# Moving a norm out of the delta rule's pair boundaries, and half panels ahead of the SSD diagonals

## The chip, the cores and the metric

The kernel runs on one core of a Trainium2 chip. The metric is the device time of one execution in microseconds, the median over several. The core has five engines, each with its own instruction queue, kept in step by semaphores: TensorE (PE in the profile, its weight loads PEld), VectorE (DVE), ScalarE (ACT), GpSimd (POOL) and SyncE (SP, which issues the DMAs here).

## The reference

Two transformer blocks over 512 tokens of width 1024. The change is in the mixer of the second block, which projects its input, runs a gated delta rule over 8 heads and an SSD (Mamba-2) scan over 16 heads, and joins both:

```python
z = h @ w_in                     # split into q, k, v, z_a, ..., z_s, x_s, b_s, c_s, dt_s
qkv = silu(causal_dwconv(concat([q, k, v]), gdn_conv_w))
o_a = gdn_chunked(q, k, v, g, beta)                    # 8 heads of 128
o_a = rms_norm(o_a, gdn_norm_w) * silu(z_a)            # mean of squares over a head's 128
xbc = silu(causal_dwconv(concat([x_s, b_s, c_s]), ssd_conv_w, ssd_conv_b))
y = ssd_chunked(xs, dt, a_neg, bm, cm) + ssd_d * xs    # 16 heads of 64
o_s = rms_norm(y * silu(z_s), ssd_norm_w)
mix = concat([o_a, o_s]) @ w_out
```

The norm of `o_a` needs, for each head and token, the sum of 128 squares, a root, an inverse, and this one number spread over the head's 128 rows.

## The kernel before

Everything is kept transposed: 128 channels on the partitions, 512 tokens along the free dimension. A projection goes panel by panel. A panel is 128 output channels: 8 blocks of depth, each multiplied three times (upper weights by upper input, upper by lower, lower by upper), so 24 matmuls of 128x512 into one PSUM bank. SP loads a panel's raw weights, ACT rounds them to the upper part (`upper_part`, L471), DVE subtracts to the lower part (`lower_parts`, L455); four panels are in flight (`RING`), and the banks `ps0` to `ps3` rotate.

The order on each engine is the order of the code. In the second block's mixer PE runs `gdn_project_pe` (24 panels with small work behind them), `gdn_pe`, the 12 panels of `ssd_xbc` and one of `ssd_dt`, `ssd_pe`, `y_turn_pe`, the 8 panels of `ssd_z`, then `out2_pe`.

`gdn_pe`, `gdn_act`, `gdn_dve` and `gdn_pool` are the delta rule. They take the 8 heads two at a time (four pairs); for each pair they go through a list of stages, each stage for the one head and then for the other. `PE_STAGES` is: `bc` (spread the head's decays and betas over the partitions), `kk` (products of keys with keys and with queries), `t0` and the six levels of a blocked inversion (`x`, `u`, `t` for each), `w`, the scan over four chunks (`v`, `s`), then `ss` and `bk`. ACT has `dec` (the decays, Exp), `small`, copies, then `sq` (keeps the output, and squares it) and `rt` (root). DVE has `kb`, `at`, `qk`, the levels, the states, then `inv` and `out`. `after(engine, stage, n)` gives the semaphore count at which a stage of head n is through. The norm of a pair's output stands at the pair's end:

- ACT `sq` (L1697, L1698) squares; PE `ss` (L1656) sums over the partitions with four matmuls of one column; ACT `rt` (L1703) takes four roots for a head; DVE `inv` (L1754) inverts; PE `bk` spreads over 128 rows by `spread` (L634: four 128x128 matmuls); DVE `out` (L1757) multiplies.
- The next pair's first stage, `bc`, waits for `out` of the head two before it.

The profile counts a float32 matmul as two instructions, so `ss` of two heads is x16, and so is `spread` of two heads.

`ssd_pe` first runs `ssd_prepare_pe` (turns blocks of `xbc`, with halves of the panels 0 to 2 of `gdn_z` in between: `z_half_pe`, L1794 to L1796, 12 matmuls for a half panel). Then for each of 16 heads: PE `broadcast` (L1894, L428), ACT four Exp (L1961), DVE the mask product (L1990), PE `diag` (L1903), ACT keeps (L1954). A half panel of `gdn_z` stands behind `diag(n)` for the six n in `Z_IN_DIAG`. `z_keep_dve`, `z_upper_act` and `z_silu_act` handle these panels, on DVE behind heads 6 and 11, on ACT behind heads 2, 7 and 12 (upper parts) and 8 (Silu).

Of the kernel before, what the change touches and what calls it, by code (L numbers as in the profile page):

```python
# [126 lines left out]
def build(nc, T, stop_at=None):  # L127
# [1381 lines left out]
    NL = len(LEVELS)  # L1509
    lev = [(k, l) for l in range(NL) for k in ("x", "u", "t") if k != "t" or l < NL - 1]  # L1510
    scan = [(k, c) for c in range(QB) for k in ("v", "s")]
    PE_STAGES = ["bc", "kk", "t0"] + lev + ["w"] + scan + ["ss", "bk"]
    ACT_STAGES = ["dec", "small", "t0"] + [x for x in lev if x[0] != "u"] + ["w"] + [("v", c) for c in range(QB)] + ["sq", "rt"]
    DVE_STAGES = ["kb", "at", "qk"] + [("u", l) for l in range(NL - 1)] + ["full", ("u", NL - 1)] + [("s", c) for c in range(QB)] + ["inv", "out"]
    POOL_STAGES = ["q", "vb"] + [("c", l) for l in range(NL - 1)] + ["kbe", "kd"]
    STAGES = {"pe": PE_STAGES, "act": ACT_STAGES, "dve": DVE_STAGES, "pool": POOL_STAGES}

    def after(eng, stage, n):

        order_ = STAGES[eng]  # L1520
        return n // 2 * 2 * len(order_) + 2 * order_.index(stage) + n % 2 + 1

    def slots(n):

        return [solve_t[:, n % 2, k, :] for k in range(6)]

    def heads_in_turn(stages):
        for n2 in range(4):
            for stage in stages:
                for n in (2 * n2, 2 * n2 + 1):  # L1530
                    yield stage, stage[0] if isinstance(stage, tuple) else stage, n

    def packed(x, half):

# [10 lines left out]
        return qkv[:, 8 + n, :]  # L1545

    def gdn_pool(pool):
        for stage, what, n in heads_in_turn(POOL_STAGES):
            vb, kt = chunks(qkv[:, 16 + n, :]), chunks(ktok[:, n, :])
            if stage == "q":  # L1550

                pool.wait_ge(g_act, after("act", "dec", n))
                pool.wait_ge(g_pe, after("pe", "kk", n))
                pool.tensor_tensor(qkv[:, n, :], qkv[:, n, :], slots(n)[3], ALU.mult).then_inc(g_pool, 1)
                continue
            if stage == "vb":
# [16 lines left out]
            pool.tensor_tensor(packed(*level_part(n, l)), packed(slots(n)[0], 0),  # L1573
                               per_chunk(cst[:, C_LEV + (l + 1) * 64:C_LEV + (l + 2) * 64]), ALU.mult).then_inc(g_pool, 1)

    def gdn_pe(pe):
        for stage, what, n in heads_in_turn(PE_STAGES):
            At, Tm, U, X, C, QK = slots(n)
            B = [ps[4 * (n % 2) + k] for k in range(4)]
            q, k, vb, kd = qkv[:, n, :], qkv[:, 8 + n, :], qkv[:, 16 + n, :], ktok[:, n, :]  # L1580
# [2 lines left out]
            if stage == "bc":  # L1583

                if n >= 2:
                    pe.wait_ge(g_dve, after("dve", "out", n - 2))
                else:
                    pe.wait_ge(small_act, 2)
                    pe.wait_ge(small_dve, 2)
# [40 lines left out]
            elif stage == "w":  # L1630
                pe.wait_ge(g_dve, after("dve", ("u", NL - 1), n))
                pe.wait_ge(g_pool, after("pool", "kbe", n))
                for c in range(QB):
                    mm = pe.matmul(B[0][:, cc[c]], C[:, cc[c]], U[:, cc[c]], start=True, stop=True)
            elif what == "v":
                c = stage[1]
                if c == 0:
                    pe.wait_ge(g_act, after("act", "w", n))
                    pe.wait_ge(g_pool, after("pool", "kd", n))
                else:  # L1640
                    pe.wait_ge(g_dve, after("dve", ("s", c - 1), n))
                mm = pe.matmul(B[1][:, cc[c]], U[:, cc[c]], vb[:, cc[c]], start=True, stop=c == 0)
                if c:
                    mm = pe.matmul(B[1][:, cc[c]], X[:, cc[c]], S, start=False, stop=True)
            elif what == "s":
                c = stage[1]
                pe.wait_ge(g_act, after("act", ("v", c), n))
                if c:
                    pe.matmul(B[2][:, cc[c]], S, q[:, cc[c]], start=True, stop=False)
                mm = pe.matmul(B[2][:, cc[c]], Tm[:, cc[c]], QK[:, cc[c]], start=c == 0, stop=True)  # L1650
                if c < QB - 1:
                    mm = pe.matmul(B[3][:, cc[c]], kd[:, cc[c]], Tm[:, cc[c]], start=True, stop=True)
            elif stage == "ss":
                pe.wait_ge(g_act, after("act", "sq", n))
                for c in range(QB):
                    mm = pe.matmul(B[0][:, c:c + 1], X[:, cc[c]], ones[:, 0:1], start=True, stop=True)  # L1656
            elif stage == "bk":
                pe.wait_ge(g_dve, after("dve", "inv", n))
                mm = spread(pe, B[1], stat[:, 48 + 4 * (n % 2):52 + 4 * (n % 2)], QB)
            mm.then_inc(g_pe, 1)  # L1660

    def gdn_act(act):
        for stage, what, n in heads_in_turn(ACT_STAGES):
            At, Tm, U, X, C, QK = slots(n)
            B = [ps[4 * (n % 2) + k] for k in range(4)]
            cc = [slice(c * P, (c + 1) * P) for c in range(QB)]
# [25 lines left out]
            elif what == "v":  # L1692
                act.wait_ge(g_pe, after("pe", stage, n))
                x = act.activation(Tm[:, cc[stage[1]]], B[1][:, cc[stage[1]]], ACT.Copy)
            elif stage == "sq":
                act.wait_ge(g_pe, after("pe", ("s", QB - 1), n))
                act.activation(qkv[:, n, :], B[2][:, :], ACT.Copy)  # L1697
                x = act.activation(X, B[2][:, :], ACT.Square)  # L1698
            elif stage == "rt":
                act.wait_ge(g_pe, after("pe", "ss", n))  # L1700
                for c in range(QB):
                    o = 40 + 4 * (n % 2) + c
                    x = act.activation(stat[:, o:o + 1], B[0][:, c:c + 1], ACT.Sqrt, bias=QEPS[:, c, n:n + 1], scale=1.0 / 128)  # L1703
            x.then_inc(g_act, 1)

    def gdn_dve(dve, st):
        for stage, what, n in heads_in_turn(DVE_STAGES):
            At, Tm, U, X, C, QK = slots(n)
            B = [ps[4 * (n % 2) + k] for k in range(4)]
            q, k = qkv[:, n, :], qkv[:, 8 + n, :]  # L1710
# [31 lines left out]
            elif what == "s":  # L1742
# [6 lines left out]
                                                 op0=ALU.mult, op1=ALU.add)  # L1749
                else:  # L1750
                    x = dve.tensor_copy(stat[:, 92:93], stat[:, 95:96])
            elif stage == "inv":
                dve.wait_ge(g_act, after("act", "rt", n))
                x = dve.reciprocal(stat[:, 48 + 4 * (n % 2):52 + 4 * (n % 2)], stat[:, 40 + 4 * (n % 2):44 + 4 * (n % 2)])  # L1754
            elif stage == "out":
                dve.wait_ge(g_pe, after("pe", "bk", n))
                x = dve.scalar_tensor_tensor(out=q, in0=q, scalar=v(V_GDN), in1=B[1][:, :], op0=ALU.mult, op1=ALU.mult)  # L1757
            x.then_inc(g_dve, 1)
            dve.wait_ge(g_dve, after("dve", stage, n))

# [93 lines left out]

    s_turn_in = [xbc[:, b, :] for b in range(10)]
    s_turn_out = [xt[:, b, :] for b in range(10)]
    Z_IN_DIAG = {1: (3, 0), 4: (3, 1), 6: (4, 0), 9: (4, 1), 11: (5, 0), 14: (5, 1)}
    Z_IN_STATE = ((6, 0), (6, 1), (7, 0), (7, 1))

    def ssd_prepare_pe(pe):  # L1860
# [25 lines left out]
    def ssd_pe(pe):  # L1886
# [23 lines left out]
        for n in range(16):  # L1910
            if 1 <= n < 15:
                broadcast(n + 1)
            diag(n)
            if n in Z_IN_DIAG:
                z_half_pe(pe, *Z_IN_DIAG[n])
        for c in range(QB):
            for g in range(2):
                e = 2 * c + g
# [342 lines left out]
    with block as blk:  # L2261
# [28 lines left out]
        def _(pe):  # L2290
# [31 lines left out]
            gdn_project_pe(pe)  # L2322
            pe.wait_ge(tok2_done, 16)
            gdn_pe(pe)
            pe.wait_ge(g_dve, after("dve", "out", 7))
            for name in ("ssd_xbc", "ssd_dt"):
                multiply(pe, name, u_of(u_hi), u_of(u_lo))
            ssd_pe(pe)
            y_turn_pe(pe)
            multiply(pe, "ssd_z", u_of(u_hi), u_of(u_lo))  # L2330
# [8 lines left out]
        def _(act):  # L2339
# [73 lines left out]
        def _(dve):  # L2413
# [113 lines left out]
```

## Time and profile before

| | |
|---|---|
| median of 3 runs | 2531.75 us (2530.27 to 2535.05) |
| the profiled execution: time, span | 2535.12 us, 2533.3 us |
| PE busy, share of the span | 2428.6 us, 96% |
| DVE busy | 1340.2 us, 53% |
| ACT busy | 886.5 us, 35% |
| POOL busy | 120.7 us, 5% |
| mean granted TensorE clock | 0.973 |

Times inside the trace are microseconds from the start of the span. The granted clock is given as a share of 2.4 GHz: 1.00 is 2.4 GHz, 0.50 is 1.2 GHz, and a value in between is a stretch that had some of each. PE's busy time counts matmuls that overlap in its pipeline, so the start of one matmul to the start of the next is what a matmul costs in a stream. A timeline row may merge several instructions; x16 says how many.

### The profile page before, as it was taken

Reading aid. Unit: us, or ns where it says so; the run is one execution under the profiler, and the core shown is the slowest. Engines: PE = TensorE matmul, PEld = TensorE weight load, DVE = VectorE, ACT = ScalarE, POOL = GpSimd, SP = SyncE. Lnnn points to the kernel's source line nnn. Section 1 sums busy time; section 2 is a strip of 40 time slices with the busy share of each in tenths; the row PEclk is TensorE's granted clock in tenths of the full one; section 3 lists DMA queues with packets and bytes.
Section 4 is the critical chain, followed back from the end, with each engine's and each line's share of the span. In section 5 each row is a group of like instructions: output and inputs, shape, how many; then the busy total and the mean of one; then the engine's idle time right before and its main releaser. Section 6 shows DMA issues by size and latency. Waiting matters only on the chain.

```text
span 2533.3 us, 31667 instructions
## 1 busy us (share of the span) xinstructions
PE 2428.6 (96%) x12764; PEld 1900.3 (75%) x12764; DVE 1340.2 (53%) x2037; ACT 886.5 (35%) x1480; POOL 120.7 (5%) x156
## 2 busy tenths in 40 slices
PE   7999999999999999999999999888998999999997
PEld 6888888887556658888888667677876687788886
DVE  5454335436466557544533586344464754777623
ACT  4222223321344455322222454443345243433321
POOL 0000000000012220000000000233000000000000
PEclk9999999999999999999999999898998999999998
DMA  5333324330221125333333232000031232333331
GB/s 168 100 93 97 98 80 137 97 83 17 76 66 59 39 71 171 88 100 93 99 98 82 80 91 76 2 2 2 27 85 34 58 100 67 92 92 100 99 95 48
DMA packets 372465, 200.02 MB, mean 79 GB/s; under 512 B 12000, under 2 KB 364512, under 8 KB 372320
## 3 DMA queue, kind: packets, MB, share of 16 engines
q1 hardware_dynamic: 372320, 198.01, 27.1%
q8 instruction: 101, 1.65, 0.3%
q14 instruction: 44, 0.36, 0.0%
HBM read 190.38 MB, written 7.60 MB: 78 GB/s over the span
## 4 chain that ended last, share of the span: by engine, by line
PE 91%; DVE 6%; ACT 2%; issue 1%; POOL 0%; DMA 0%; DVEq 0%; SPq 0%; ACTq 0%; POOLq 0%
PE ps L522 19%; PE ps L523 19%; PE ps L524 19%; PE ps L376 2%; PE ps L1025 2%; PE ps L1433 2%; PE ps L1435 2%; PE ps L1434 2%; PE ps L1061 2%; PE ps L378 2%; PE ps L377 2%; PE ps L2137 1%; PE ps L2139 1%; PE ps L2138 1%; PE ps L912 1%
## 5 line engine op out<-in xcount | busy, mean ns | idle before, releaser
L455 DVE TENSOR_TENSOR w_lo<-w_raw,w_hi 128x1024 fp32r<-128x1024 f32 (+2 forms) x366 | 422.7, 1156 | 310.4 <-ACT w_hi L471 309.2
L522 PE MATMUL ps<-u_hi,w_hi 128*128 128x512 f32 (+1 forms) x1416 | 557.5, 394 | 3.0 <-DVE w_lo L455 2.1
L523 PE MATMUL ps<-u_lo,w_hi 128*128 128x512 f32 (+1 forms) x1416 | 555.0, 392 | 0.0
L524 PE MATMUL ps<-u_hi,w_lo 128*128 128x512 f32 (+1 forms) x1416 | 554.6, 392 | 0.0
L471 ACT ACTIVATE w_hi<-w_raw 128x1024 fp32r<-128x1024 f32 (+2 forms) x366 | 366.2, 1002 | 502.5 <-PE ps L524 438.4
L522 PEld LDWEIGHTS ps<-u_hi,w_hi 128*128 128x128 f32 (+1 forms) x1416 | 264.2, 187 | 64.3 <-DVE w_lo L455 3.0
L524 PEld LDWEIGHTS ps<-u_hi,w_lo 128*128 128x128 f32 (+1 forms) x1416 | 264.2, 187 | 60.9 <-issue 1.5
L523 PEld LDWEIGHTS ps<-u_lo,w_hi 128*128 128x128 f32 (+1 forms) x1416 | 264.1, 187 | 60.4 <-issue 2.2
L524 PE MATMUL ps<-mid_hi,w_lo 128*128 128x512 f32 x528 | 208.6, 395 | 0.0
L522 PE MATMUL ps<-mid_hi,w_hi 128*128 128x512 f32 x528 | 208.6, 395 | 0.0
L523 PE MATMUL ps<-mid_lo,w_hi 128*128 128x512 f32 x528 | 208.5, 395 | 0.0
L523 PEld LDWEIGHTS ps<-mid_lo,w_hi 128*128 128x128 f32 x528 | 99.1, 188 | 24.2
L524 PEld LDWEIGHTS ps<-mid_hi,w_lo 128*128 128x128 f32 x528 | 99.1, 188 | 24.0
L522 PEld LDWEIGHTS ps<-mid_hi,w_hi 128*128 128x128 f32 x528 | 99.1, 188 | 24.0
L646 ACT ACTIVATE pair_a<-pair_a 128x512 f32<-128x512 f32 x44 | 27.9, 635 | 214.6 <-DVE pair_a L655 214.6
L1126 POOL TENSOR_TENSOR probs<-probs,stat 128x256 f32<-128x256 f32 (+1 forms) x80 | 56.1, 706 | 871.6 <-DVE stat L1135 871.6
L660 DVE TENSOR_TENSOR part<-ps,pair_b 128x512 f32<-128x512 f32 x44 | 30.4, 692 | 126.6 <-PE ps L524 126.5
L376 PE MATMUL ps<-u_hi,w_hi 128*128 128x512 f32 x192 | 89.3, 465 | 0.0
L1309 DVE SCALAR_TENSOR_TENSOR conv_t<-conv_in,vec,conv_t 128x512 f32<-128x512 f32 x108 | 81.0, 750 | 9.0 <-ACT conv_t L1291 6.4
L2223 ACT ACTIVATE conv_t<-conv_in,vec 128x512 f32<-128x512 f32 x44 | 36.0, 818 | 138.9 <-DVE conv_in L2238 138.9
L655 DVE TENSOR_TENSOR pair_a<-ps,rms 128x512 f32<-128x512 f32 x44 | 30.4, 691 | 95.5 <-PE ps L524 95.4
L378 PE MATMUL ps<-u_hi,w_lo 128*128 128x512 f32 x192 | 77.4, 403 | 0.0
(440 smaller groups left out, 3680.9 us busy)
## 6 DMA issues: line engine op xcount, KB each, us to landing
w_raw<-w_in_dram SPq DMA_DIRECT2D x101, 512.0 KB, 3.8
w_raw<-ffn_w_gate_dram SPq DMA_DIRECT2D x44, 512.0 KB, 3.8
w_raw<-ffn_w_up_dram SPq DMA_DIRECT2D x44, 512.0 KB, 3.8
w_raw<-w_up_dram SPq DMA_DIRECT2D x44, 512.0 KB, 3.8
w_raw<-ffn_w_down_dram SPq DMA_DIRECT2D x32, 512.0 KB, 4.0
w_raw<-w_out_dram SPq DMA_DIRECT2D x24, 512.0 KB, 3.8
w_raw<-w_down_dram SPq DMA_DIRECT2D x16, 512.0 KB, 3.7
w_raw<-ffn_w_down_dram SPq DMA_DIRECT2D x16, 384.0 KB, 3.4
```

The costliest lines, as they stand in the source:

```text
L376: pe.matmul(out, wh, u_hi[:, k, :], start=k == 0, stop=False)
L377: pe.matmul(out, wh, u_lo[:, k, :], start=False, stop=False)
L378: mm = pe.matmul(out, wl, u_hi[:, k, :], start=False, stop=k == DK - 1)
L455: dve.tensor_tensor(lo, raw, hi.bitcast(F32), ALU.subtract).then_inc(w_split, 1)
L471: act.activation(w_hi[:, n % RING, 0:blocks, 0:cols], w_raw[:, n % RING, 0:blocks, 0:cols], ACT.Copy).then_inc(hi_done, 1)
L522: pe.matmul(out, wh, h_k, start=k0 + k == 0, stop=False)
L523: pe.matmul(out, wh, l_k, start=False, stop=False)
L524: mm = pe.matmul(out, wl, h_k, start=False, stop=end)
L1025: mm = pe.matmul(bank[:, 0:w], j.q[:, q * P:(q + 1) * P], j.k[:, 0:w], start=True, stop=plain)
L1061: mm = pe.matmul(out[:, j.first[t]:SEQ], j.v[t], x, start=t == 0, stop=t == nk - 1)
L1126: pool.tensor_tensor(x, x, r, ALU.mult).then_inc(sc_norm, 1)
L1309: dve.scalar_tensor_tensor(out=t, in0=x, scalar=v(wcol + block(n) * taps + k), in1=t, op0=ALU.mult, op1=ALU.add).then_inc(conv_done if k = ...
```

## The change

Four things are done.

1. The stages `ss` and `bk` leave the end of PE's list. `ss` of heads n-2 and n-1 is now issued behind `kk` of the pair n, n+1, writes into the bank B[1], and reads squares that `sq` puts into `upper(n)` and no longer into X. `bc` waits for `sq` of the head two before, not for `out`.
2. `rt`, `inv` and `out` are gone from the stage lists. DVE has a stage `mean` behind `qk` of the next pair: one instruction on 128x4 numbers for a head, that adds sum/128 to `QEPS`. The last pair's `ss` and `mean` stand by themselves at the end. One root (`o_root_act`) and one reciprocal (`o_inverse_dve`) then serve all eight heads (128x32).
3. The panels of `ssd_xbc` get a loop of their own (`xbc_pe`): behind each of the first eight panels one head's `spread` is issued, into ps6 or ps7, and behind that panel's convolution on DVE the multiplication (`o_norm_dve`) of that head.
4. In the SSD, the half panels of `gdn_z` are issued ahead of `diag(n)`, not behind it, and the first one at n = 0 where it was 1.

```diff
-    PE_STAGES = ["bc", "kk", "t0"] + lev + ["w"] + scan + ["ss", "bk"]
-    ACT_STAGES = ["dec", "small", "t0"] + [x for x in lev if x[0] != "u"] + ["w"] + [("v", c) for c in range(QB)] + ["sq", "rt"]
-    DVE_STAGES = ["kb", "at", "qk"] + [("u", l) for l in range(NL - 1)] + ["full", ("u", NL - 1)] + [("s", c) for c in range(QB)] + ["inv", "out"]
+    PE_STAGES = behind(["bc", "kk", "t0"] + lev + ["w"] + scan, ("kk", "ss"))
+    ACT_STAGES = ["dec", "small", "t0"] + [x for x in lev if x[0] != "u"] + ["w"] + [("v", c) for c in range(QB)] + ["sq"]
+    DVE_STAGES = behind(["kb", "at", "qk"] + [("u", l) for l in range(NL - 1)] + ["full", ("u", NL - 1)] + [("s", c) for c in range(QB)],
+                        ("qk", "mean"))
+    NEXT_PAIR = ("ss", "mean")
+    TURNS = {eng: [(stage, n) for pair in range(5) for stage in stages
+                   for n in (2 * pair, 2 * pair + 1) for n in (n - 2 if stage in NEXT_PAIR else n,) if 0 <= n < 8]
+             for eng, stages in STAGES.items()}
...
                 if n >= 2:
-                    pe.wait_ge(g_dve, after("dve", "out", n - 2))
+                    pe.wait_ge(g_act, after("act", "sq", n - 2))
...
             elif stage == "ss":
-                pe.wait_ge(g_act, after("act", "sq", n))
+                pe.wait_ge(g_act, after("act", "dec", n + 2) if n < 6 else after("act", "sq", n))
                 for c in range(QB):
-                    mm = pe.matmul(B[0][:, c:c + 1], X[:, cc[c]], ones[:, 0:1], start=True, stop=True)
-            elif stage == "bk":
-                pe.wait_ge(g_dve, after("dve", "inv", n))
-                mm = spread(pe, B[1], stat[:, 48 + 4 * (n % 2):52 + 4 * (n % 2)], QB)
+                    mm = pe.matmul(B[1][:, c:c + 1], upper(n)[:, cc[c]], ones[:, 0:1], start=True, stop=True)
...
-                x = act.activation(X, B[2][:, :], ACT.Square)
-            elif stage == "rt":
-                act.wait_ge(g_pe, after("pe", "ss", n))
-                for c in range(QB):
-                    o = 40 + 4 * (n % 2) + c
-                    x = act.activation(stat[:, o:o + 1], B[0][:, c:c + 1], ACT.Sqrt, bias=QEPS[:, c, n:n + 1], scale=1.0 / 128)
+                x = act.activation(upper(n), B[2][:, :], ACT.Square)
...
-            elif stage == "inv":
-                dve.wait_ge(g_act, after("act", "rt", n))
-                x = dve.reciprocal(stat[:, 48 + 4 * (n % 2):52 + 4 * (n % 2)], stat[:, 40 + 4 * (n % 2):44 + 4 * (n % 2)])
-            elif stage == "out":
-                dve.wait_ge(g_pe, after("pe", "bk", n))
-                x = dve.scalar_tensor_tensor(out=q, in0=q, scalar=v(V_GDN), in1=B[1][:, :], op0=ALU.mult, op1=ALU.mult)
+            elif stage == "mean":
+                dve.wait_ge(g_pe, after("pe", "ss", n))
+                x = dve.scalar_tensor_tensor(out=QEPS[:, :, n], in0=B[1][:, 0:QB], scalar=1.0 / 128, in1=QEPS[:, :, n], op0=ALU.mult, op1=ALU.add)
...
+    def o_root_act(act):
+        act.wait_ge(g_dve, after("dve", "mean", 7))
+        act.activation(o_means, o_means, ACT.Sqrt).then_inc(o_rt, 1)
+
+    def o_inverse_dve(dve):
+        dve.wait_ge(o_rt, 1)
+        dve.reciprocal(o_means, o_means).then_inc(o_inv, 1)
+
+    def o_spread_pe(pe, n):
+        pe.wait_ge(o_inv, 1)
+        if n >= 2:
+            pe.wait_ge(o_normed, n - 1)
+        spread(pe, ps[6 + n % 2], QEPS[:, :, n], QB).then_inc(o_bc, 1)
+
+    def o_norm_dve(dve, n):
+        if n < 8:
+            x = o_a[:, n, :]
+            dve.wait_ge(o_bc, n + 1)
+            dve.scalar_tensor_tensor(out=x, in0=x, scalar=v(V_GDN), in1=ps[6 + n % 2][:, :], op0=ALU.mult, op1=ALU.mult).then_inc(o_normed, 1)
...
+    def xbc_pe(pe):
...
+            mm.then_inc(w_used, 1)
+            if p < 8:
+                o_spread_pe(pe, p)
...
-    Z_IN_DIAG = {1: (3, 0), 4: (3, 1), 6: (4, 0), 9: (4, 1), 11: (5, 0), 14: (5, 1)}
+    Z_IN_DIAG = {0: (3, 0), 4: (3, 1), 6: (4, 0), 9: (4, 1), 11: (5, 0), 14: (5, 1)}
...
-            diag(n)
             if n in Z_IN_DIAG:
                 z_half_pe(pe, *Z_IN_DIAG[n])
+            diag(n)
...
-            pe.wait_ge(g_dve, after("dve", "out", 7))
-            for name in ("ssd_xbc", "ssd_dt"):
-                multiply(pe, name, u_of(u_hi), u_of(u_lo))
+            pe.wait_ge(g_dve, after("dve", "mean", 7))
+            xbc_pe(pe)
+            multiply(pe, "ssd_dt", u_of(u_hi), u_of(u_lo))
...
             gdn_act(act)
+            o_root_act(act)
...
-            conv_dve(dve, "ssd_xbc", 24, 4, V_SCW)
+            o_inverse_dve(dve)
+            conv_dve(dve, "ssd_xbc", 24, 4, V_SCW, lambda p: o_norm_dve(dve, p))
```

## Rows read from the trace of the kernel before

**Rows 1.** The page, chain of work that ended last: shares by engine.

```profile
PE 91%; DVE 6%; ACT 2%; issue 1%; POOL 0%; DMA 0%; DVEq 0%; SPq 0%; ACTq 0%; POOLq 0%
```

**Rows 2.** Timeline between second and third pair: start, duration, engine, line, operation, count, idle before.

```profile
1691.67 2.03 PE L1656 MATMUL ps<-cst,solve_t 128*128 128x1 f32 x16 [0.54 <-ACT solve_t L1698]
1691.99 0.62 ACT L1698 ACTIVATE solve_t<-ps 128x512 f32<-128x512 f32 x1
1692.62 1.28 ACT L1703 ACT_TABLE_LOAD   x1
1694.97 3.46 PE L634 MATMUL ps<-cst,stat 128*128 128x128 f32 x16 [1.26 <-DVE stat L1754]
1698.26 0.38 PE L1590 MATMUL ps<-cbf 128*128 128x512 bf16 x1
1699.33 0.60 ACT L1670 ACTIVATE solve_t<-ps 128x512 f32<-128x512 f32 x1 [2.79 <-PE ps L428]
```

**Rows 3.** Chain of waits, the two other boundaries: start, duration, what.

```profile
1636.68 0.49 ACT solve_t L1698
...
1646.04 0.60 ACT solve_t L1670
...
1745.31 0.60 ACT qkv L1697
...
1755.26 0.60 ACT solve_t L1670
```

**Rows 4.** Timeline from the last pair's end into `ssd_xbc`.

```profile
1801.53 0.62 ACT L1698 ACTIVATE solve_t<-ps 128x512 f32<-128x512 f32 x1
...
1804.28 0.18 DVE L1754 RECIPROCAL stat<-stat 128x4 f32<-128x4 f32 x1 [3.34 <-ACT stat L1703]
...
1809.20 0.79 PE L522 MATMUL ps<-u_hi,w_hi 128*128 128x512 f32 x1 [0.91 <-DVE qkv L1757]
...
1814.04 0.40 PE L524 MATMUL ps<-u_hi,w_lo 128*128 128x512 f32 x1
...
1817.45 0.39 PE L524 MATMUL ps<-u_hi,w_lo 128*128 128x512 f32 x1
```

**Rows 5.** Windows: length, busy times of PE, PEld, DVE, ACT, POOL; PEclk, DMA, GB/s.

```profile
1810.00:1812.00 2.00, 2.00 (x6) 1.51 (x6) 0.00 (x0) 0.00 (x0) 0.00 (x0) 0.50 0.00 0
...
1820.00:1875.00 55.00, 55.00 (x244) 45.56 (x243) 39.62 (x52) 23.53 (x31) 0.00 (x0) 1.00 0.33 89
...
1902.00:1904.00 2.00, 2.00 (x14) 1.67 (x13) 1.97 (x4) 1.99 (x4) 0.00 (x0) 1.00 0.00 0
...
1944.00:1946.00 2.00, 2.00 (x8) 1.71 (x8) 1.26 (x3) 0.38 (x1) 0.00 (x0) 0.50 0.00 0
```

**Rows 6.** Timeline, the same spread of two heads inside `out2`.

```profile
2052.87 1.95 PE L634 MATMUL ps<-cst,stat 128*128 128x128 f32 x16
...
2054.57 0.47 PE L2137 MATMUL ps<-oa_hi,w_hi 128*128 128x512 f32 x1
```

**Rows 7.** Groups by line in 1809 to 1882, the convolution's steps on DVE.

```profile
L1309 DVE SCALAR_TENSOR_TENSOR conv_t<-conv_in,vec,conv_t 128x512 f32<-128x512 f32 x36 | 27.0, 750 | 1.5 <-ACT conv_t L1291 0.7
```

**Rows 8.** Timeline of the SSD diagonals.

```profile
1903.17 5.77 DVE L1981 TENSOR_TENSOR xt<-xt,sv 128x512 f32<-128x512 f32 x8
...
1912.86 1.83 PE L1903 MATMUL ps<-xt,pair_b 128*128 128x64 f32 x8 [3.48 <-DVE pair_b L1990]
...
1917.46 1.05 ACT L471 ACTIVATE w_hi<-w_raw 128x1024 fp32r<-128x1024 f32 x1
...
1921.10 0.39 PE L1894 MATMUL ps<-cbf 128*128 128x512 bf16 x1
1921.54 1.00 PE L1903 MATMUL ps<-xt,pair_b 128*128 128x64 f32 x8
...
1942.80 1.97 PE L1903 MATMUL ps<-xt,pair_b 128*128 128x64 f32 x8 [3.65 <-DVE pair_b L1990]
...
1948.58 0.39 PE L1894 MATMUL ps<-cbf 128*128 128x512 bf16 x1
```

More of the change, by code:

```diff
@@ L1511, in build, with behind, heads_in_turn @@
     scan = [(k, c) for c in range(QB) for k in ("v", "s")]
-    PE_STAGES = ["bc", "kk", "t0"] + lev + ["w"] + scan + ["ss", "bk"]
-    ACT_STAGES = ["dec", "small", "t0"] + [x for x in lev if x[0] != "u"] + ["w"] + [("v", c) for c in range(QB)] + ["sq", "rt"]
-    DVE_STAGES = ["kb", "at", "qk"] + [("u", l) for l in range(NL - 1)] + ["full", ("u", NL - 1)] + [("s", c) for c in range(QB)] + ["inv", "out"]
+    def behind(stages, *later):
+        out = []
+        for stage in stages:
+            out += [stage] + [x for spot, x in later if spot == stage]
+        return out
+    PE_STAGES = behind(["bc", "kk", "t0"] + lev + ["w"] + scan, ("kk", "ss"))
+    ACT_STAGES = ["dec", "small", "t0"] + [x for x in lev if x[0] != "u"] + ["w"] + [("v", c) for c in range(QB)] + ["sq"]
+    DVE_STAGES = behind(["kb", "at", "qk"] + [("u", l) for l in range(NL - 1)] + ["full", ("u", NL - 1)] + [("s", c) for c in range(QB)],
+                        ("qk", "mean"))
     POOL_STAGES = ["q", "vb"] + [("c", l) for l in range(NL - 1)] + ["kbe", "kd"]
     STAGES = {"pe": PE_STAGES, "act": ACT_STAGES, "dve": DVE_STAGES, "pool": POOL_STAGES}
+    NEXT_PAIR = ("ss", "mean")
+    TURNS = {eng: [(stage, n) for pair in range(5) for stage in stages
+                   for n in (2 * pair, 2 * pair + 1) for n in (n - 2 if stage in NEXT_PAIR else n,) if 0 <= n < 8]
+             for eng, stages in STAGES.items()}
+    PLACE = {(eng, stage, n): i + 1 for eng, turns in TURNS.items() for i, (stage, n) in enumerate(turns)}
     def after(eng, stage, n):
-        order_ = STAGES[eng]
-        return n // 2 * 2 * len(order_) + 2 * order_.index(stage) + n % 2 + 1
+        return PLACE[eng, stage, n]
     def slots(n):
         return [solve_t[:, n % 2, k, :] for k in range(6)]
[L1527 to L1531, printed above, removed]
+    def heads_in_turn(eng):
+        for stage, n in TURNS[eng]:
+            yield stage, stage[0] if isinstance(stage, tuple) else stage, n
     def packed(x, half):
@@ L1547, in gdn_pool @@
     def gdn_pool(pool):
-        for stage, what, n in heads_in_turn(POOL_STAGES):
+        for stage, what, n in heads_in_turn("pool"):
             vb, kt = chunks(qkv[:, 16 + n, :]), chunks(ktok[:, n, :])
@@ L1576, in gdn_pe @@
     def gdn_pe(pe):
-        for stage, what, n in heads_in_turn(PE_STAGES):
+        for stage, what, n in heads_in_turn("pe"):
             At, Tm, U, X, C, QK = slots(n)
@@ L1653, in gdn_pe @@
             elif stage == "ss":
-                pe.wait_ge(g_act, after("act", "sq", n))
+                pe.wait_ge(g_act, after("act", "dec", n + 2) if n < 6 else after("act", "sq", n))
                 for c in range(QB):
-                    mm = pe.matmul(B[0][:, c:c + 1], X[:, cc[c]], ones[:, 0:1], start=True, stop=True)
-            elif stage == "bk":
-                pe.wait_ge(g_dve, after("dve", "inv", n))
-                mm = spread(pe, B[1], stat[:, 48 + 4 * (n % 2):52 + 4 * (n % 2)], QB)
+                    mm = pe.matmul(B[1][:, c:c + 1], upper(n)[:, cc[c]], ones[:, 0:1], start=True, stop=True)
             mm.then_inc(g_pe, 1)
     def gdn_act(act):
-        for stage, what, n in heads_in_turn(ACT_STAGES):
+        for stage, what, n in heads_in_turn("act"):
             At, Tm, U, X, C, QK = slots(n)
@@ L1697, in gdn_act @@
                 act.activation(qkv[:, n, :], B[2][:, :], ACT.Copy)
-                x = act.activation(X, B[2][:, :], ACT.Square)
-            elif stage == "rt":
-                act.wait_ge(g_pe, after("pe", "ss", n))
-                for c in range(QB):
-                    o = 40 + 4 * (n % 2) + c
-                    x = act.activation(stat[:, o:o + 1], B[0][:, c:c + 1], ACT.Sqrt, bias=QEPS[:, c, n:n + 1], scale=1.0 / 128)
+                x = act.activation(upper(n), B[2][:, :], ACT.Square)
             x.then_inc(g_act, 1)
     def gdn_dve(dve, st):
-        for stage, what, n in heads_in_turn(DVE_STAGES):
+        for stage, what, n in heads_in_turn("dve"):
             At, Tm, U, X, C, QK = slots(n)
@@ L1758, in gdn_dve @@
             x.then_inc(g_dve, 1)
             dve.wait_ge(g_dve, after("dve", stage, n))
+    o_rt, o_inv, o_bc, o_normed = (sem("o_" + n) for n in ("root", "inverse", "spread", "normed"))
+    o_means = QEPS.rearrange("p c h -> p (c h)")
+    def o_root_act(act):
[4 more added lines that the diff above has]
+        dve.reciprocal(o_means, o_means).then_inc(o_inv, 1)
@@ new lines, in o_spread_pe @@
+    def o_spread_pe(pe, n):
[9 more added lines that the diff above has]
+    def xbc_pe(pe):
+        s = segs["ssd_xbc"]
+        for p in range(12):
+            n = s.base + p
+            pe.wait_ge(w_split, n + 1 + RING)
+            pe.wait_ge(bank_read, s.group + p + 1)
+            out = ps[(s.group + p) % BANKS][:, :]
+            for k in range(DK):
+                wh, wl = w_hi[:, n % RING, k, :], w_lo[:, n % RING, k, :]
+                pe.matmul(out, wh, u_hi[:, k, :], start=k == 0, stop=False)
+                pe.matmul(out, wh, u_lo[:, k, :], start=False, stop=False)
+                mm = pe.matmul(out, wl, u_hi[:, k, :], start=False, stop=k == DK - 1)
+            mm.then_inc(w_used, 1)
+            if p < 8:
+                o_spread_pe(pe, p)
```

## The prediction

> **What bounds the kernel now.** I read the page's chain first: 91% of it is PE, 6% DVE, 2% ACT [rows 1]. So almost everywhere PE's stream is the time, and what can be won is where PE stands still or runs at the lower clock. The mixer of the second block has such places, and the change touches two kinds of them.
>
> The first is the end of each pair of heads in the delta rule. In the timeline between the second and third pair [rows 2] the reader sees a relay: ACT's last square ends at 1692.61, PE sums, ACT loads the root's table (1.28), DVE inverts, PE spreads (from 1694.97, 16 instructions in 3.46), DVE multiplies, and only then does PE start the next pair's broadcasts (1698.26) and ACT its decays (1699.33). The chain of waits shows the same at the two other boundaries [rows 3]. At the end of the last pair the relay goes from 1802.15 to 1809.20, where the projection `ssd_xbc` starts [rows 4]. Its first 11 matmul spacings, from 1809.20 to 1814.04, are 0.44 us each; 15 later ones, to 1817.45, are 0.227. The windows say why: granted clock 0.50 in 1810 to 1812, which is 1.2 GHz, after an engine that had largely waited [rows 5].
>
> The second is the SSD's diagonals. PE is idle for 3.48 us ahead of the first `diag` (1912.86) and for 3.65 ahead of the one at 1942.80 (ACT is then busy with the Silu of the z panels, between two table loads), and each time it works at 1.2 GHz for a while behind the gap [rows 5, 8].
>
> **Part 1: the three boundaries between pairs.** `bc` will wait for `sq` of the head two before. That is done where `ss` starts now, 1691.67. From `bc`'s first matmul to the decays it takes 1699.33 - 1698.26 = 1.07 [rows 2]. So the decays start at 1692.74 (ACT is free from 1692.61) and not at 1699.33: 6.6 us. At the first boundary the first square ends at 1636.68 + 0.49 = 1637.17; with 0.05 for the handover and 1.07 the decays start at 1638.29, not 1646.04: 7.75. At the third the copy starts at 1745.31, the square 0.60 later and lasts about 0.5, so the decays start at 1747.5, not 1755.26: 7.75 [rows 3]. What follows the decays is unchanged, and each pair's own length stays. Sum: 22.1. No new table load comes in: ACT's Copy and Square run with Exp's table in place, since no load stands before them [rows 2].
>
> `ss` and `mean` come back in the next pair. `ss` of two heads costs 2.03 of PE [rows 2], behind `kk`, where PE has to wait anyway for DVE's `at` and for GpSimd's first mask; `t0` may start up to 1.4 later, and it has more than that before its consumer's mask is ready. `mean` costs DVE twice about 0.2 (the reciprocal of 128x4 takes 0.18 [rows 4]), just when ACT and PE do the first `x` and `u`. I take 0 for both; if that cover fails it is up to 2.4 for each pair, 7.2 in all.
>
> **Part 2: the last pair's end.** ACT's last square ends at 1802.15 [rows 4]. `ss` of head 7 is half of 2.03, so 1803.2; `mean` 0.2 and two handovers: PE starts `ssd_xbc` at 1803.55 and not at 1809.20: 5.65. The root (load 1.28 and one short instruction) and the reciprocal then run under the first panel, 24 x 0.227 = 5.45, and the first spread is behind that panel: no wait.
>
> With a gap of under half a microsecond in place of the relay, I expect PE to keep 2.4 GHz into the projection. That gives back 4.84 - 11 x 0.227 = 2.35.
>
> By the Trainium skill (TensorE: Matmul & The Clock Gate, Part 1, What's actually happening), the default state is the throttled one and activity releases it. The windows of rows 5 agree in direction, 0.50 behind the relay; by this rule, too, the 2.35 would be gained.
>
> **Part 3: the spreads move into the projection.** Eight spreads now stand in PE's full stream, so they cost their whole price. Inside `out2`, in a full stream, two cost 2054.57 - 2052.87 = 1.70 [rows 6]; with a little for changing over twice as often, 0.9 each: 7.2 lost. Upper bound: what the relay shows at 1.2 GHz, 3.46 for two, so 13.8 for eight. I take 7.2, since the stream around is like that of rows 6. DVE's multiplication, the same kind of instruction as a convolution step (750 ns [rows 7]), is hidden: in 1820 to 1875 DVE is busy for 39.6 of 55 [rows 5], so 72% of a panel's 5.45, 3.9, and with the multiplication 4.7 against PE's 5.45 + 0.9. No spread waits for its bank: the multiplication two heads back is long done.
>
> **Part 4: half panels ahead of the diagonals.** A half panel is 12 x 0.227 = 2.73.
> - The first one moves in front of `diag(0)`. PE's previous piece ended at 1912.86 - 3.48 = 1909.38, and DVE's scaling (`xt`), which it must await, ended at 1908.94 [rows 8]. So it runs to 1912.1, inside the gap, and takes the idleness away that let the clock fall. Then, at 2.4 GHz, `diag(0)` 0.9, broadcast 0.44, `diag(1)` 0.9: the next broadcast starts at 1915.1 and not at 1921.10: 6.0.
> - The half panel behind head 9 moves ahead of it, into the 3.65 gap: 2.73. And the stretch behind the gap, 1942.80 to 1948.58, is 5.78 for a `diag` and a half panel that at 2.4 GHz are 3.6: 2.15. Against it stands the rounding of a weight panel on ACT (1.05 at 1917.46), which was hidden under the first half panel and is now in line with the decays: -1.0. Together 3.9. The other half panels only swap places with a `diag` that had to wait for the same products.
>
> I followed the three queues through all 16 heads with these durations; no further wait appears. Sum: 9.9. Lower bound: only the first half panel's 2.73 is hidden and the clock falls as before.
>
> **Sum.** 22.1 + 5.65 + 2.35 - 7.2 + 9.9 = 32.8. The profiled execution took 2535.12, so it would be 2502.3. That execution is at the top of the three runs; their median is 2531.75, and 2531.75 - 32.8 gives 2499.0. What follows the diagonals is a PE stream that waits for no load, so nothing gives it back. A difference of 0.2% (5 us) is about what a measurement of this kernel can tell from none.
>
> **The rivals.**
> - *The clock takes some back.* A pair's length, from its decays to its last square, is 1691.67 - 1646.04 = 45.6 for the second and 1746.4 - 1699.33 = 47.1 for the third [rows 2, 3]: 1.5 depends on where the lower clock falls. The three pairs now start at other phases. Lost at worst 1.5 each, and a fall at `ssd_xbc` costs the 2.35 as well: 2506. It could also gain up to 1.5. Chance 0.12.
> - *The z half panels buy only what they cover.* If ACT's decays, not PE, set the pace of the diagonals, moving PE work inside them gives only the 2.73 ahead of `diag(0)` and perhaps its clock (3.3), so 4 to 7 us less than I expect: 2499 + 5 = 2504. For it speaks that every head goes through four decays on ACT between its broadcast and its `diag`; against it, that each half panel stands between a broadcast and the next, so that ACT waits as well. Chance 0.14.
> - *Spreads at 1.2 GHz.* As in rows 2: 13.8 and not 7.2, so 2505.6. Against it: transposes of the same size stand between half panels in 1902 to 1904 at 1.00 [rows 5]. Chance 0.03.
> - *Slower: the projection loses the clock.* If the small matmuls between the panels made PE fall to 1.2 GHz throughout, `ssd_xbc` (288 matmuls) would pay 288 x (0.44 - 0.227) = 61, and the time would be about 2560 or more. It decides against the change from some 155 matmuls at the lower clock, where the 32.8 are used up. Chance 0.02. The Trainium skill (TensorE: Matmul & The Clock Gate, Why this matters for your kernels) warns that thin matmuls let the clock oscillate at each step of the depth; the window 1902 to 1904, with small pieces between and 1.00, does not bear that out for a stream without gaps.
> - *The boundary doesn't get shorter*, because some other engine is behind when `bc` comes early. ACT is free, DVE idle, GpSimd has finished its part of the pair, and `row_g` is ready. Chance 0.02.
>
> **How the numbers follow.** Forecast 0.67; the rivals 0.12, 0.14, 0.03, 0.02 and 0.02. Its own range is 2495 to 2502 (clock 1.5 or so either way, scatter of the runs 2). For 8 in 10 I reach up to the first two rivals and down by the clock's gain: 2493 to 2507. Faster 0.96, same 0.015 (a boundary that stays, with a weak part 4), slower 0.025.
>
> **What would show it.** Part 1: decays about 1.1 behind the first square's end at three boundaries, no table load there, and the chain without L634 in the delta rule. Part 2: from last square to the first matmul of `ssd_xbc` 1.4, with spacing 0.227 from the start. Part 3: eight spreads, each 0.9, and PE without idle time in the projection, which lasts 7 longer than its panels. Part 4: no PE gap over 2 us in the diagonals, clock 1.00 throughout, and from the first `diag` to the last some 10 less than now. The prediction is wrong if the lower clock shows up inside the projection, if `t0` waits for `ss`, or if DVE's `mean` sits on the chain.

## The result and the profile after

The median of five runs is 2515.40 us (2506.05 to 2516.47), against 2531.75 before (2530.27 to 2536.21, five runs by now): the ratio is 0.9921, 95% interval 0.9904 to 0.9937. The change is a gain of about 20 by the ratio (16 by the medians), where 32.8 were forecast, and the time lies above the stated range.

The profiled execution of the changed kernel is the fastest of its five, 2506.05 with a span of 2504.2. That is 29.1 under the span of before, but 9.4 of it were there before the changed part began: the first pair's decays start at 1580.09, those of before at 1589.52, and all code ahead of them is the same. So I compare stage by stage, never end by end. The page's chain is as in [rows 1]:

```profile
span 2504.2 us, 31628 instructions
...
PE 91%; DVE 6%; ACT 2%; issue 1%; DMA 0%; POOL 0%; DVEq 0%; SPq 0%; ACTq 0%
```

The chain of waits of the changed kernel at the three boundaries answers to [rows 2, 3]: output copy, square, broadcasts, decays.

```profile
1627.88 0.60 ACT qkv L1704
1628.48 0.50 ACT qkv L1705
1629.41 0.66 PE ps L428 x3
1630.10 0.60 ACT solve_t L1677
...
1674.66 0.60 ACT qkv L1704
...
1676.88 0.60 ACT solve_t L1677
...
1724.86 0.60 ACT qkv L1704
...
1727.08 0.60 ACT solve_t L1677
```

From the copy to the next decays it is 2.22 each time; before it was 9.96, 8.79 and 9.95. The relay is gone and with it two table loads at each boundary (the root's, and the one that brought Exp back behind it): 22.0 saved, where 22.1 was worked out.

The timeline at the last pair's end answers to [rows 4]:

```profile
1776.08 0.62 ACT L1705 ACTIVATE qkv<-ps 128x512 f32<-128x512 f32 x1
1776.71 1.28 ACT L1766 ACT_TABLE_LOAD   x1
1777.29 0.17 DVE L1756 SCALAR_TENSOR_TENSOR gs<-ps,gs 128x4 f32<-128x4 f32 x1 [1.80 <-PE ps L1666]
1777.92 0.17 DVE L1756 SCALAR_TENSOR_TENSOR gs<-ps,gs 128x4 f32<-128x4 f32 x1 [0.46 <-PE ps L1666]
1778.12 0.23 ACT L1766 ACTIVATE gs<-gs 128x32 f32<-128x32 f32 x1
1778.14 0.80 PE L1793 MATMUL ps<-u_hi,w_hi 128*128 128x512 f32 x1 [0.33 <-DVE gs L1756]
...
1781.24 0.40 PE L1794 MATMUL ps<-u_lo,w_hi 128*128 128x512 f32 x1
```

Last square's end (1776.70) to the first matmul of `ssd_xbc`: 1.44, with PE idle for only 0.33 ahead of it. But the seven spacings up to 1781.24 are 0.44 on average: PE is at 1.2 GHz here in spite of the short gap, for 3.1 instead of 4.8.

The stages side by side, in microseconds, each from the start of the first instruction named to the start of the second (for the diagonals: first `diag` to the state's first product on DVE):

| stage | before | changed | forecast of the difference | difference |
|---|---|---|---|---|
| four pairs, decays to output copy | 46.6, 44.5, 46.0, 44.8 | 47.8, 44.6, 48.0, 47.6 | 0 | +6.0 |
| three boundaries | 28.7 | 6.7 | -22.1 | -22.0 |
| last copy to `ssd_xbc` | 9.12 | 3.51 | -5.65 | -5.6 |
| `ssd_xbc` and `ssd_dt` | 73.19 | 79.79 | +4.85 | +6.6 |
| first z half to first `diag` | 30.47 | 30.36 | 0 | -0.1 |
| diagonals | 51.63 | 47.32 | -9.9 | -4.3 |
| states and turns, to `ssd_z` | 31.79 | 31.81 | 0 | 0 |
| `ssd_z` to the end | 537.0 | 536.8 | 0 | -0.2 |

Sum of the differences: -19.6. The waits behave as worked out to 0.1; the 13 that are missing are in three rows, 6.0 in the pairs, 5.6 in the diagonals and 1.75 in the projection.

The windows of the changed kernel show what those rows have in common. Columns as in [rows 5]; the first three rows are its pairs 2, 3 and 4 from decays to copy, the fourth is the diagonals:

```profile
1630.10:1674.66 44.56, 39.92 (x677) 35.59 (x677) 19.89 (x44) 15.94 (x46) 16.08 (x18) 0.96 0.01 2
1676.88:1724.86 47.98, 43.06 (x677) 38.97 (x677) 20.34 (x44) 15.94 (x47) 15.95 (x18) 0.86 0.01 2
1727.08:1774.63 47.55, 42.39 (x677) 38.76 (x677) 20.05 (x44) 15.93 (x46) 15.99 (x18) 0.89 0.01 2
1888.29:1935.61 47.32, 42.54 (x216) 34.62 (x216) 16.55 (x23) 27.01 (x80) 0.00 (x0) 0.82 0.13 34
```

The three pairs have the same instructions and the same sums behind `kk`, and there is 3.4 between the shortest and the longest: the granted clock is 0.96 in the short one and 0.86 in the long one. In the diagonals it is 0.82.

### The profile page after: what moved, and what is told of

It reads as the page before. It is cut to its first block, busy times and chain, and to the rows that moved or that the text cites. A ratio compares the mean times of both kernels' runs of the same rounds, so it can differ in the third digit from the quotient of the medians.

```text
span 2504.2 us, 31628 instructions
## 1 busy us (share of the span) xinstructions
PE 2415.1 (96%) x12764; PEld 1894.1 (76%) x12764; DVE 1340.5 (54%) x2038; ACT 873.1 (35%) x1443; POOL 120.2 (5%) x156
## 4 chain that ended last, share of the span: by engine, by line
PE 91%; DVE 6%; ACT 2%; issue 1%; DMA 0%; POOL 0%; DVEq 0%; SPq 0%; ACTq 0%
PE ps L522 19%; PE ps L523 19%; PE ps L524 19%; PE ps L1025 2%; PE ps L376 2%; PE ps L1433 2%; PE ps L1435 2%; PE ps L1434 2%; PE ps L1061 2%; PE ps L378 2%; PE ps L377 2%; PE ps L2175 1%; PE ps L2177 1%; PE ps L2176 1%; PE ps L912 1%; PE ps L1793 1%
## 5 line engine op out<-in xcount | busy, mean ns | idle before, releaser
L522 PE MATMUL ps<-u_hi,w_hi 128*128 128x512 f32 (+1 forms) x1320 | 518.5, 393 | 2.1 <-DVE w_lo L455 2.1
L523 PE MATMUL ps<-u_lo,w_hi 128*128 128x512 f32 (+1 forms) x1320 | 516.1, 391 | 0.0
L524 PE MATMUL ps<-u_hi,w_lo 128*128 128x512 f32 (+1 forms) x1320 | 515.9, 391 | 0.0
L522 PEld LDWEIGHTS ps<-u_hi,w_hi 128*128 128x128 f32 (+1 forms) x1320 | 245.6, 186 | 58.8 <-DVE w_lo L455 3.0
L523 PEld LDWEIGHTS ps<-u_lo,w_hi 128*128 128x128 f32 (+1 forms) x1320 | 245.5, 186 | 56.3 <-issue 1.9
L524 PEld LDWEIGHTS ps<-u_hi,w_lo 128*128 128x128 f32 (+1 forms) x1320 | 245.4, 186 | 56.4 <-issue 0.6
L376 PE MATMUL ps<-u_hi,w_hi 128*128 128x512 f32 x192 | 86.6, 451 | 0.0
L1433 PE MATMUL ps<-u_hi,w_hi 128*128 128x512 f32 x192 | 77.1, 402 | 0.0
```

The source lines that it names most:

```text
L376: pe.matmul(out, wh, u_hi[:, k, :], start=k == 0, stop=False)
L522: pe.matmul(out, wh, h_k, start=k0 + k == 0, stop=False)
L523: pe.matmul(out, wh, l_k, start=False, stop=False)
L524: mm = pe.matmul(out, wl, h_k, start=False, stop=end)
L1433: pe.matmul(out, wh, u_hi[:, k, :], start=k == 0, stop=False)
```

## The experiments

All ran beside the kernel before, which took 2530.48, 2535.59 or 2534.67 there, so kernels of different sections are compared by their ratios to it and not by their medians. Theory A: the missing time is TensorE at 1.2 GHz. Theory B: the sums and means lie on the path. Theory C: the unchanged first block merely happened to be short in the one profile. Theory D: the diagonals are long by waits of their own.

**The same kernel again.**

> The changed kernel once more, for a second profile of the same code. Theory A (the boundaries are as short as worked out, and what is missing is TensorE time at 1.2 GHz that now falls into the pairs' own stages and into the diagonals): median about 2515; the three boundaries (last pair's output copy to the next decays) 2.2 each as in the first profile; pairs from decays to output copy between 44.5 and 48, the longer ones with more time at 1.2 GHz inside. Theory B (the sums behind the next pair's products lie on the path): all pairs longer than before by the same amount, whatever the clock. Theory C (the first block, which is not changed, merely fell differently in the one profile): decays of the first pair at 1580 or at 1589.5 from run to run.

Median 2511.19 (2510.64 to 2515.85), ratio 0.9924 [0.9912, 0.9937]. Boundaries 2.2 each, pairs 48.0, 46.1, 48.0, 47.6, diagonals 47.36, first decays at 1583.24. These are A's numbers. C had expected a start at 1580 or at 1589.5, and it was between: in the thirteen profiles of all kernels it lay anywhere from 1580.1 to 1590.1. That is as much as the executions of one kernel scatter, though with one profile of each it isn't shown that it is the cause; it explains none of the missing 13, which are counted behind it.

**The two halves of the change alone.** `norm_only` has the half panels where they were before:

```diff
-    Z_IN_DIAG = {0: (3, 0), 4: (3, 1), 6: (4, 0), 9: (4, 1), 11: (5, 0), 14: (5, 1)}
+    Z_IN_DIAG = {1: (3, 0), 4: (3, 1), 6: (4, 0), 9: (4, 1), 11: (5, 0), 14: (5, 1)}
...
-            if n in Z_IN_DIAG:
-                z_half_pe(pe, *Z_IN_DIAG[n])
             diag(n)
+            if n in Z_IN_DIAG:
+                z_half_pe(pe, *Z_IN_DIAG[n])
```

> The norm's four relays moved as in the change, z half panels left behind the diagonals as before. By the prediction's own terms 22.1 + 5.65 + 2.35 - 7.2 = 22.9, so 2509. Theory A: some 6 of it is lost to the clock in the pairs and about 2 at the projection's start, so 2516 to 2519. Theory B: about the same time, but with the pairs equally long.

Median 2519.02, ratio 0.9949 [0.9936, 0.9962]: 13 of the 22.9. In its profile the boundaries are 2.2 each and the diagonals 51.7; the four pairs (48.8, 45.7, 45.7, 45.9) are 4.2 longer than before, and from `ssd_xbc` to the first `diag` it takes 8.05 more, where 4.85 was worked out. `z_only` is the kernel before with these lines the other way round.

> The kernel before with only the z half panels ahead of the diagonals. By the prediction 9.9, so 2522. Theory A: diagonals shorter by 4 to 5 since the clock falls inside them again, so 2527 to 2528; profile: first diag to the first state product 47, not 51.6, with two or three stretches at 0.50.

Median 2522.58, ratio 0.9965 [0.9953, 0.9977], a gain of 9. By the medians this is what the prediction had said (2522), and my expectation from theory A was wrong. The diagonals took 41.03, even less than the 41.7 worked out; 0.9 came back in the turns behind them. So the same reordering, on the same instructions, gives 10.6 without the norm's move and 4.3 with it. The two timelines, PE's `diag` only, first of `z_only`:

```profile
1911.79 1.10 PE L1903 MATMUL ps<-xt,pair_b 128*128 128x64 f32 x8 [0.65 <-DVE pair_b L1990]
...
1915.29 1.10 PE L1903 MATMUL ps<-xt,pair_b 128*128 128x64 f32 x8 [0.69 <-DVE pair_b L1990]
...
1917.55 1.10 PE L1903 MATMUL ps<-xt,pair_b 128*128 128x64 f32 x8 [0.72 <-DVE pair_b L1990]
```

and of the changed kernel:

```profile
1888.29 1.10 PE L1941 MATMUL ps<-xt,pair_b 128*128 128x64 f32 x8 [0.67 <-DVE pair_b L2028]
...
1891.79 1.10 PE L1941 MATMUL ps<-xt,pair_b 128*128 128x64 f32 x8 [0.68 <-DVE pair_b L2028]
...
1894.04 1.97 PE L1941 MATMUL ps<-xt,pair_b 128*128 128x64 f32 x8 [0.71 <-DVE pair_b L2028]
```

For 5.75 from the first `diag` on they agree to 0.01, with the same gaps of 0.7 ahead of three of the first four. Then one of them does the fourth at 1.2 GHz and the other at 2.4. No wait differs up to there; what is done in the stretch doesn't decide it alone. Length times granted clock is 39.4 in `z_only` (41.03 at 0.96) and 38.8 in the changed kernel (47.32 at 0.82), so the lower clock can carry the whole difference.

**Without the sums of heads 0 to 5.** These heads are then normed with the root of the small constant alone.

```diff
-                   for n in (n - 2 if stage in NEXT_PAIR else n,) if 0 <= n < 8]
+                   for n in (n - 2 if stage in NEXT_PAIR else n,) if (6 if stage in NEXT_PAIR else 0) <= n < 8]
```

> The changed kernel without the sums and means of heads 0 to 5 (those heads are normed with the root of the small constant alone; the last pair's stay). Theory A: the pairs keep lengths between 44.5 and 48 that go with the clock, time within 3 of the changed kernel's. Theory B (sums in line with the pairs): each of pairs 2 to 4 shorter by about 2, in all 6 less, so 2509.

Median 2510.69, ratio 0.9919 [0.9904, 0.9934]; pairs 47.8, 44.6, 48.0, 47.5, the lengths of the changed kernel to 0.1. B falls. The changed kernel's timeline shows the cover: `ss` runs from 1636.47, and `t0`, kept back until 1638.24, still leaves PE idle for 0.91 ahead of the first `x`, which waits for GpSimd.

```profile
1636.47 1.84 PE L1666 MATMUL ps<-cst,qkv 128*128 128x1 f32 x16
...
1638.24 0.68 PE L1614 MATMUL ps<-cst,qkv 64*64 64x64 f32 x16
...
1641.24 1.98 PE L1629 MATMUL ps<-solve_t 64*64 64x64 f32 x32 [0.91 <-POOL solve_t L1583]
...
1643.99 0.36 DVE L1756 SCALAR_TENSOR_TENSOR gs<-ps,gs 128x4 f32<-128x4 f32 x2
```

**A shift.** Needless matmuls in the changed kernel ahead of the projection, 8 or 4:

```diff
     def xbc_pe(pe):
         s = segs["ssd_xbc"]
+        pe.wait_ge(bank_read, s.group + 1)
+        for _ in range(8):
+            pe.matmul(ps[s.group % BANKS][:, :], identb, cbf[:, 2 * P:6 * P], start=True, stop=True)
```

> The changed kernel with 8 needless matmuls of 128x512 (1.8 at 2.4 GHz) ahead of the first panel of ssd_xbc; nothing behind it changes. If the diagonals' length is set by their own waits alone (theory D), they stay at 47.3 and the time is 1.8 longer. If it is a matter of where the lower clock's decision falls (theory A, from the comparison of the changed kernel with the half panels alone, whose instructions are the same up to the fall), the diagonals take another length between 41 and 52, and the time moves by anything from -5 to +6.

Work was added, and the median is 2510.26, ratio 0.9902 [0.9889, 0.9915], not slower than the changed kernel. The diagonals, 100 us later and with no instruction changed, took 41.00 and not 47.32, at a granted clock of 0.96 and not 0.82:

```profile
1894.14:1935.14 41.00, 36.05 (x213) 29.71 (x216) 16.55 (x23) 27.02 (x80) 0.00 (x0) 0.96 0.15 39
1901.85:1905.85 4.00, 4.00 (x27) 3.46 (x26) 0.69 (x1) 1.52 (x6) 0.00 (x0) 1.00 0.00 0
1914.90:1918.20 3.30, 3.30 (x9) 2.58 (x8) 0.29 (x1) 3.27 (x9) 0.00 (x0) 0.50 0.00 0
```

The second row lies as far behind the first `diag` as 1896 to 1900 does in the changed kernel, where the clock is 0.50. D falls: it is where the stretch lies in time against the falls of the clock. In the three profiles with 41.0 (`z_only`, `shift8`, and `fill` below) the first fall comes about 20.6 behind the first `diag`, in the three with 47.3 to 47.4 (the changed kernel twice and `no_sums`) about 5.5. The eight matmuls themselves cost 3.0 here, not 1.8, since PE was at 1.2 GHz for a part of them.

> The changed kernel with 4 needless matmuls (0.9) ahead of ssd_xbc. With 8 the diagonals went from 47.3 to 41.0. Theory A: 4 give one of the lengths seen so far (41 or 47) or one between; a length of their own waits can't change at all.

2508.18, ratio 0.9895 [0.9878, 0.9912]; diagonals 42.23, a length between.

**PE kept busy in the diagonals.** The three z panels by blocks, one or two ahead of every head:

```diff
-            if n in Z_IN_DIAG:
-                z_half_pe(pe, *Z_IN_DIAG[n])
+            for b in range(Z_UP_TO[n - 1] if n else 0, Z_UP_TO[n]):
+                z_block_pe(pe, 3 + b // 8, b % 8)
             diag(n)
...
+    Z_UP_TO = (4, 5, 6, 7, 8, 9, 11, 12, 14, 16, 17, 19, 20, 22, 24, 24)
```

> The changed kernel with the three z panels given out evenly: 4 blocks ahead of the first diagonal, then one or two blocks (3 matmuls each) ahead of every head, so that PE hardly waits. Work of PE: 16 x 1.31 + 24 x 0.68 = 37.4. Theory A: the clock stays at 1.00 and first diag to first state product is 38 to 40, so 7 to 9 less than the changed kernel's 47.3: 2503 to 2506. Theory D (ACT sets the pace): 44 or more.

Median 2501.19 (2498.28 to 2508.25), ratio 0.9871 [0.9855, 0.9887]. The diagonals take 38.31, against about 37.3 of PE's own work (an estimate: 16 x 1.31 + 24 x 0.68):

```profile
1897.35:1935.66 38.31, 35.71 (x213) 30.01 (x216) 16.48 (x23) 27.59 (x80) 0.00 (x0) 0.96 0.16 42
```

The clock of 0.96 is that of `z_only`, which took 41.03 with it. So of the 9.0 that this stretch is shorter than in the changed kernel, 2.7 are waits that are filled, and 6.3 are what a luckier place in time had given as well; that the even order keeps the clock up by itself is not shown. The stage behind, up to `ssd_z`, took 33.5 and not 31.8, so 1.7 came back.

**PE kept busy in the pairs.** Twelve needless matmuls a pair, where PE waits:

```diff
+                broadcast_row(pe, B[2][:, :], row_b, 8, n, SEQ, True, True).then_inc(g_pe, 1)
+                for _ in range(6 * (n % 2)):
+                    pe.matmul(B[3][:, :], identb, cbf[:, 2 * P:6 * P], start=True, stop=True)
+                continue
             elif stage == "kk":
...
+                mm.then_inc(g_pe, 1)
+                if n % 2:
+                    pe.wait_ge(g_act, after("act", "dec", n))
+                for _ in range(6 * (n % 2)):
+                    pe.matmul(B[1][:, :], identb, cbf[:, 2 * P:6 * P], start=True, stop=True)
+                continue
             elif stage == "t0":
```

> The changed kernel with needless matmuls where PE waits in the delta rule: 6 of 128x512 (1.3) behind the second broadcast, 6 behind the second kk, ahead of the sums. Theory A: fewer falls of the clock in the levels, pairs near 44.5 and not 48, so 6 to 10 less: 2503 to 2509. If PE's waits in this part aren't what the fall hangs on, or the filler delays t0: same or up to 4 x 1.3 more.

Median 2499.91 (2492.41 to 2506.52), ratio 0.9860 [0.9839, 0.9881]. There is more work in it, and by the ratios it takes some 15 less than the changed kernel. Its windows, pairs 2 and 3:

```profile
1628.32:1672.84 44.52, 41.19 (x688) 35.63 (x689) 19.88 (x44) 15.94 (x47) 16.09 (x18) 1.00 0.01 2
1675.06:1719.58 44.52, 42.19 (x688) 36.70 (x689) 19.89 (x44) 15.94 (x47) 16.08 (x18) 0.96 0.01 2
```

The four pairs take 45.7, 44.5, 44.5 and 44.8, 179.5 together and 8.4 less than in the changed kernel; its diagonals, moved in time by that, took 41.00. The second of the two pairs has some lower clock in it (0.96) and is as short as the first, so not every fall costs time.

**Both together.**

> Both of the last two. Theory A: the gains add, 2496 to 2500, which is where the prediction stood (2499), with pairs near 44.5, diagonals 38 to 40, and the clock at 1.00 through the diagonals.

Median 2498.92 (2491.68 to 2504.53), ratio 0.9850 [0.9831, 0.9869]: the best of all, clearly ahead of both kernels. It beats `fill` alone by less than the intervals can tell. Pairs 46.5, 44.5, 44.5, 45.8; diagonals 39.9 at a clock of 0.91, where I had expected 1.00.

**The kernel before with filler.** The same needless matmuls in it:

> The kernel before with the same needless matmuls behind the second broadcast and the second kk. If the lower clock in the pairs is something the change brought, the pairs stay at their 44.5 to 47.8 and the time is the same as before. If it was there before as well (theory A), pairs near 44.5 to 46 and 2 to 8 less than the kernel before: 2523 to 2529.

Median 2528.49 of 12 runs, ratio 0.9983 [0.9972, 0.9994]; pairs 45.6, 44.5, 44.5, 44.8.

```profile
1644.77:1689.28 44.51, 39.59 (x672) 33.74 (x672) 19.56 (x42) 15.98 (x46) 16.09 (x18) 1.00 0.01 2
```

So the lower clock in the pairs was there before the change: the filler gains 4 by the ratio, and its four pairs take 179.5. In the profile of the kernel before they take 181.9; in those of `z_only` and `z_first`, whose pairs are the same, 186.1 and 186.5. Without filler but with the norm moved, seven profiles have 186.1 to 189.9, 188.2 on average. So the profile that all was compared with very likely had short pairs by luck: against the mean of the three, 184.8, the pairs grew by about 3.4 with the change, and not by 6.0.

**The first half panel alone**, ahead of `diag(0)` in the kernel before:

> The kernel before with only the first half panel moved, ahead of diag(0); the five others stay behind their diagonals. The prediction put 6.0 of 9.9 on this one: first diag to first state product 45.6, not 51.6. Theory A allows another 2 or so either way by where the clock falls: 43 to 48, time 2524 to 2528.

Median 2531.84 of 12 runs, ratio 0.9984 [0.9974, 0.9993], a gain of 4; the profile's diagonals took 47.32, so 4.3 less, where 6.0 was worked out.

## Why the prediction was wrong

Right, by its own steps:
- The boundaries (22.1 forecast, 22.0 measured) and the last pair's end (5.65 and 5.6).
- The cover for `ss` and `mean`: taken at 0, and 0 by the run without them.
- The spreads' price. From one spread to the next in the changed kernel's chain is 6.37, a panel of 24 x 0.227 and 0.91; forecast 0.9. The root was in time for the first spread.

```profile
1785.29 0.89 PE ps L634 x8
...
1791.66 0.89 PE ps L634 x8
```

- Part 4's queues, in size: 51.6 - 9.9 = 41.7 for the diagonals at 2.4 GHz throughout, and 41.0 measured in three kernels with a clock of 0.96. In the working of the 6.0 one term is not written out: 1912.1 and the three durations behind it give 1914.3 and not 1915.1. A wait of about that size was there: PE stood idle for 0.67 ahead of the first `diag`, for DVE's product.

Wrong: three steps, with one assumption under them, that the clock falls only behind a long gap, so that taking the gaps away keeps it up.
1. "What follows the decays is unchanged, and each pair's own length stays" (part 1). The waits are unchanged, the length isn't. A pair takes 44.5 at the upper clock, and up to 48.8 (first pair of `norm_only`) with the lower clock on its path. Measured +6.0 against the one profile, some 3.4 against the mean of three; the filler gives back more than either. The rival "The clock takes some back" named this, but took its bound, 1.5 a pair, from two pairs of one profile; the other profiles show 3.5 and more.
2. "So it runs to 1912.1, inside the gap, and takes the idleness away that let the clock fall" (part 4). The half panel did fill the gap, but the first fall only moved from the first `diag` to the fourth, behind gaps of 0.7, and others followed: three stretches at 1.2 GHz in 1888 to 1936.

```profile
1896.00:1900.00 4.00, 4.00 (x11) 2.98 (x9) 0.69 (x1) 1.52 (x5) 0.00 (x0) 0.50 0.02 4
1912.00:1916.00 4.00, 4.00 (x12) 3.06 (x12) 0.69 (x1) 3.97 (x11) 0.00 (x0) 0.50 0.00 0
1928.00:1931.00 3.00, 3.00 (x11) 2.43 (x11) 0.69 (x1) 1.39 (x6) 0.00 (x0) 0.50 0.00 0
```

   It gained 4.3 of the 9.9. Whether it gains 4 or 10 is a matter of the moment at which the stretch begins, as the two shifts show. The rival "The z half panels buy only what they cover" came near in size (4 to 7 less than forecast; it was 5.6), but by luck: ACT's pace was not the limit, since 38.3 is possible with the same work on ACT.
3. "I expect PE to keep 2.4 GHz into the projection" (part 2). It was at 1.2 GHz for the first 3.1 of it, and 3.1 - 7 x 0.227 = 1.5 was lost again: of the 2.35, 0.8 was had. The remaining 0.2 of this row's 1.75 is not followed up; the spreads at 0.91 are 0.1 of it.

By what the three rows of the table lack, 6.0 + 5.6 + 1.75 = 13.4, the sum would have been -19.4; the ratio says -20. That the two agree so well may be partly luck, since the pairs' 6.0 rests on the one profile. The Trainium skill (TensorE: Matmul & The Clock Gate, Part 1, What's actually happening) says that activity releases the clock and that the decision does not start with the kernel but runs freely; the first half I had used, the second speaks for what the shifts show, and it was the half that mattered here.

The rival's 2506 counted the pairs and the projection, and not the diagonals, where nearly half of the loss was.

What stays open: which of the falls a given start brings about. Three profiles of the changed kernel's own instructions (two, and the one without sums) gave diagonals of 47.3 to 47.4 each time although the mixer began at 1580.09, 1583.24 and 1584.89, and the first fall in them came about 5.5 behind the first `diag` each time. So something earlier brings them into step; none of the runs was made to show what.

## What to carry to other kernels

A wait that was taken out of a PE chain gave back its own length here, and that could be read from the timeline to a tenth; but a stretch in which PE waits again and again for short times has no one length, but anything between that at the upper clock and that with the lower one on its path, and which it will have after a shift can't be read from the one trace before. Cost such a stretch at both clocks, from several profiles, and put both ends into the range. If the stretch matters, try to hand out the independent work evenly in it, ahead of every wait and not in large pieces: that took the diagonals from 47.3 to 38.3, of which 2.7 did not hang on the clock, and gave 1.7 back behind them. Even needless matmuls in PE's waits can pay: they did, by 8 over four pairs.

## What the runs showed of the hardware

- TensorE falls to 1.2 GHz also behind gaps of only 0.7, in the diagonals, while the same instructions with the same gaps had a mean clock of 0.96 in another kernel (0.82 and 47.32 in the changed kernel, 0.96 and 41.03 in `z_only`).
- Adding 8 matmuls (3.0 in the profile) ahead of the projection made a stretch 109 later 6.3 shorter (`shift8`); the kernel's ratio was 0.9902, against 0.9921 without them.
- Six needless matmuls at two places in each pair took the four pairs from 187.9 to 179.5 (`fill`), and in the kernel before from 181.9 to 179.5 (`before_fill`).
- The executions of one kernel scatter by up to 14 here (2492.41 to 2506.52 for `fill`); the mixer's start, behind code that no kernel changed, lay between 1580.1 and 1590.1 in the thirteen profiles.
